# Linear attention on one core: the remainder from keys times state, and the block inverse applied to it

## What is computed

```python
DN_HEADS, DN_DK, DN_DV, DN_CHUNK = 8, 128, 128, 64
a = jnp.where(strict, beta[..., :, None] * kk * decay, 0.0) + jnp.eye(DN_CHUNK)
rhs = jnp.concatenate([beta[..., None] * v, (beta * jnp.exp(g))[..., None] * k], axis=-1)
sol = lax.linalg.triangular_solve(a, rhs, left_side=True, lower=True, unit_diagonal=True)
u_t, w = sol[..., :dv], sol[..., dv:]
attn = jnp.einsum('bhnid,bhnjd->bhnij', q, k) * decay
q_g = q * jnp.exp(g)[..., None]
k_d = k * jnp.exp(g_last[..., None] - g)[..., None]

def step(state, xs):
    u_tc, w_c, attn_c, qg_c, kd_c, gl_c = xs
    u = u_tc - jnp.einsum('bhcd,bhde->bhce', w_c, state)
    o = jnp.einsum('bhcd,bhde->bhce', qg_c, state) + jnp.einsum('bhij,bhje->bhie', attn_c, u)
    state = jnp.exp(gl_c)[..., None, None] * state + jnp.einsum('bhcd,bhce->bhde', kd_c, u)
    return state, o
```

## Time and profile before

| what | value |
|---|---|
| median of 3 runs | 1782.01 us |
| the 3 runs | 1780.25, 1787.84, 1782.01 us |
| span of the profiled execution | 1783.6 us |
| PE busy | 1706.6 us (96%) |
| DVE busy | 703.0 us (39%) |
| ACT busy | 465.0 us (26%) |
| POOL busy | 140.3 us (8%) |
| turning of values of head 0 to head 7 (L711, first and last) | 179.3 to 344.1 us from the span's start |
| PE waits for a DMA of expert weights, both layers | 21.5 us in 29 waits |

### The profile page before, as it was taken

How to read it: one execution, slowest core, us unless ns; L and a number is a source line. 1 busy time by engine, 2 the same in 40 slices (tenths; PEclk the granted TensorE clock), 3 DMA queues, 4 the chain that set the end, 5 groups by cost and what they waited for, 6 DMA issues and landing times. The chain is left out here.

```text
span 1783.6 us, 19887 instructions
## 1 busy us (share of the span) xinstructions
PE 1706.6 (96%) x7340; PEld 829.5 (47%) x7340; DVE 703.0 (39%) x1365; ACT 465.0 (26%) x709; POOL 140.3 (8%) x192
## 2 busy tenths in 40 slices
PE   7999999998999999999998999989899999999998
PEld 4555666643334434433345565565343443433343
DVE  4788444415333433333322103355333433333231
ACT  5666244412101011000124716653101101001020
POOL 0035710000000000000000101100000000000000
PEclk9999999999999999999999999999899999999999
DMA  8122232385999999999951020045899999999941
GB/s 280 51 81 74 79 83 71 110 326 201 426 426 427 426 426 427 427 427 429 410 217 48 1 103 0 1 189 218 346 427 426 427 427 426 427 427 429 427 168 47
DMA packets 85113, 481.06 MB, mean 270 GB/s; under 512 B 22320, under 2 KB 39472, under 8 KB 58416
## 3 DMA queue, kind: packets, MB, share of 16 engines
q1 hardware_dynamic: 80432, 471.64, 65.0%
q0 software_dynamic: 4608, 8.40, 1.3%
HBM read 476.33 MB, written 12.06 MB: 274 GB/s over the span
## 5 line engine op out<-in xcount | busy, mean ns | idle before, releaser
L1937 PE MATMUL bank<-ring,xT 128*64 128x512 f32 x2048 | 465.2, 600 | 22.2 <-DMA ring<-in_w 21.5
L1937 PEld LDWEIGHTS bank<-ring,xT 128*64 128x64 f32 x2048 | 142.4, 137 | 289.1 <-issue 272.0
L1889 DVE TENSOR_TENSOR H<-H,bank 128x512 f32<-128x512 f32 x240 | 154.0, 683 | 301.8 <-PE bank L1925 301.8
L1961 PE MATMUL bank<-ring,sg 128*64 128x512 f32 x1024 | 228.3, 598 | 0.3 <-ACT sg L1977 0.2
L1961 PEld LDWEIGHTS bank<-ring,sg 128*64 128x64 f32 x1024 | 70.8, 137 | 134.3 <-issue 126.3
L635 PE MATMUL bank<-ring,ring 128*128 128x512 f32 x256 | 126.9, 604 | 0.0
L620 PE MATMUL bank<-ring,ring 128*128 128x512 f32 x256 | 112.9, 593 | 0.0
L1977 ACT ACTIVATE sg<-bank 128x512 f32<-128x512 f32 x32 | 19.2, 600 | 353.1 <-PE bank L1946 353.1
L1879 DVE SCALAR_TENSOR_TENSOR low<-bank,weight_now,high 128x512 fp32r<-128x512 f32 x64 | 48.1, 751 | 159.3 <-ACT high L1983 156.0
L2305 PE MATMUL bank<-ring,ring 128*128 128x512 f32 x256 | 110.5, 592 | 0.0
L1925 PE MATMUL bank<-high,Sb 128*128 128x512 f32 x240 | 106.7, 445 | 0.0
(11 more groups left out here) (336 smaller groups left out, 2024.6 us busy)
## 6 DMA issues: line engine op xcount, KB each, us to landing
ring<-in_w SPq DMA_DIRECT2D x192, 2048.0 KB, 30.2
ring<-in_w_heads SPq DMA_DIRECT2D x16, 1024.0 KB, 5.1
ring<-in_w_ple_gate SPq DMA_DIRECT2D x4, 2048.0 KB, 32.9
ring<-in_w_kv SPq DMA_DIRECT2D x3, 2048.0 KB, 21.3
ring<-in_b_w_q SPq DMA_DIRECT2D x3, 2048.0 KB, 19.6
inverses<-ring SPq DMA_DIRECT2D x16, 256.0 KB, 4.1
ring<-inverses SPq DMA_DIRECT2D x16, 256.0 KB, 3.2
rows<-ring SPq DMA_DIRECT2D x8, 512.0 KB, 4.3
```

Of the source, the lines that this page charges most:

```text
L1889: dve.tensor_tensor(out, out, k.bank[6 + j % 2][:, :], ALU.add).then_inc(s.added, 1)
L1937: last = pe.matmul(out[e * SLOTS:(e + 1) * SLOTS, :], k.xT[:, at, e * SLOTS:(e + 1) * SLOTS], w[:, e, c, :], start=(at == 0), stop=(at == ...
L1961: last = pe.matmul(k.bank[2 + n][e * SLOTS:(e + 1) * SLOTS, :], k.hT[:, c, e * SLOTS:(e + 1) * SLOTS], w[:, e, c % 2, n * HALF:(n + 1) * H ...
```

## The change

The product W of inverse and scaled keys goes, with its copy nWT and with kb. In tile t > 0 TensorE multiplies the plain normalised keys by the state (L745 of the changed program, into bank 2, semaphore kS), VectorE adds that, times -beta e^g of the token, to vb (`remainder`, one 128x128 op, semaphore r), and V is applied to the result. A filler stands between the product and V's. beG gets its sign when it is made. The normalised keys are written to oT, whose slot of a head is free until that head's output is written, in place of the qk buffer. Wait for ln_o (ScalarE has read bank 2) joins the wait for og, and both stand ahead of tile 0.

```diff
@@ delta_semaphores, early_units
-     s.Z, s.Ts, s.W, s.nW, s.u, ...
+     s.Z, s.Ts, s.kS, s.r, s.u, ...
-                pe.wait_ge(s.nW, HEADS)
+                pe.wait_ge(s.tok, 2 * HEADS)
                 yield from unit(3, range(HEADS - 1))
@@ TensorE, keys
-                q, kk = k.qk[:, h % 2, 0, :], k.qk[:, h % 2, 1, :]
+                q, kk = k.qk[:, h % 2, 0, :], k.oT[:, h, :]
@@ TensorE, recur
-                pe.wait_ge(s.tok, 3 * h + 3)
+                pe.wait_ge(s.tok, 2 * h + 2)
                 pe.wait_ge(s.Vs, JOINS * h + JOINS)
+                wait(pe, s.og, h)
+                wait(pe, s.ln_o, h)
                 for t in range(NT):
-                    last = pe.matmul(tile(bank[6], t), k.kb[:, t, :], V[:, t, :], start=True, stop=True)
-                last.then_inc(s.W, 1)
-                wait(pe, s.og, h)
-                for t in range(NT):
-                    last = pe.matmul(tile(bank[3], t), V[:, t, :], k.vb[:, t, :], start=True, stop=(t == 0),
-                                     skip_group_check=True)
                     if t:
-                        pe.wait_ge(s.nW, h + 1)
                         pe.wait_ge(s.St, 3 * h + t)
-                        last = pe.matmul(tile(bank[3], t), tile(k.nWT[:, :], t), k.state[:, (t - 1) % 2, :],
-                                         start=False, stop=True, skip_group_check=True)
-                    last.then_inc(s.u, 1)
+                        pe.matmul(tile(bank[2], t), tile(k.oT[:, h, :], t), k.state[:, (t - 1) % 2, :], start=True,
+                                  stop=True).then_inc(s.kS, 1)
+                        take(rest, 1)
+                        pe.wait_ge(s.r, 3 * h + t)
+                    pe.matmul(tile(bank[3], t), V[:, t, :], k.vb[:, t, :], start=True, stop=True).then_inc(s.u, 1)
                     take(rest, 1)
                     pe.wait_ge(s.us, 4 * h + t + 1)
@@ VectorE
-                dve.tensor_tensor(kk, kk, k.rnorm[:, 1, :], ALU.mult).then_inc(s.qkn, 1)
+                dve.tensor_tensor(k.oT[:, h, :], kk, k.rnorm[:, 1, :], ALU.mult).then_inc(s.qkn, 1)
...
-                wait(dve, s.W, h)
...
-                for dst, scale in ((k.kb, k.beG), (k.kd, k.eGrest)):
-                    dve.tensor_tensor(dst[:, :, :], k.kt[:, h, :, :], bcast(head_of(scale, h), 2, P),
-                                      ALU.mult).then_inc(s.tok, 1)
+                dve.tensor_tensor(k.kd[:, :, :], k.kt[:, h, :, :], bcast(head_of(k.eGrest, h), 2, P),
+                                  ALU.mult).then_inc(s.tok, 1)
...
+            def remainder(h, t):
+
+                dve.wait_ge(s.tok, 2 * h + 2)
+                dve.wait_ge(s.kS, 3 * h + t)
+                dve.scalar_tensor_tensor(k.vb[:, t, :], tile(bank[2], t), head_of(k.beG, h)[:, t:t + 1], k.vb[:, t, :],
+                                         ALU.mult, ALU.add).then_inc(s.r, 1)
...  (recur, at the end of each of the three rounds that make a state)
+                    remainder(h, t + 1)
@@ ScalarE, recur
-                act.wait_ge(s.W, h + 1)
-                act.activation(k.nWT[:, :], bank[6][:, :], ACT.Copy, scale=-1.0).then_inc(s.nW, 1)
```

More of the change, by code:

```diff
@@ L515, in gates_vector_sums @@
                       k.bank[3][:, NT * HEADS:2 * NT * HEADS], G, ALU.subtract).then_inc(g.diff, 1)
-    ch.link(dve.tensor_tensor(k.beG[:, :, :], k.beta[:, :, :], k.eG[:, :, :], ALU.mult))
+    ch.link(dve.scalar_tensor_tensor(k.beG[:, :, :], k.beta[:, :, :], -1.0, k.eG[:, :, :], ALU.mult, ALU.mult))
     dve.wait_ge(g.acts, 2)
@@ L544, in delta_semaphores @@
      s.exported, s.blocks, s.init, s.inv, s.flipped, s.returned, s.C, s.tok, s.v_turned, s.X, s.Xs, s.Y, s.Vs,
-     s.Z, s.Ts, s.W, s.nW, s.u, s.us, s.dS, s.St, s.o, s.osq, s.oss, s.ln_o, s.rn_o, s.og_step, s.og, s.low, s.olow, s.w_late) = (
+     s.Z, s.Ts, s.kS, s.r, s.u, s.us, s.dS, s.St, s.o, s.osq, s.oss, s.ln_o, s.rn_o, s.og_step, s.og, s.low, s.olow, s.w_late) = (
          k.sem(f"dn_{name}") for name in
@@ L549, in delta_semaphores @@
              "zeroed", "exported", "blocks", "init", "inv", "flipped", "returned", "C", "tok", "v_turned",
-             "X", "Xs", "Y", "Vs", "Z", "Ts", "W", "nW", "u", "us", "dS", "St", "o", "osq", "oss", "ln_o",
+             "X", "Xs", "Y", "Vs", "Z", "Ts", "kS", "r", "u", "us", "dS", "St", "o", "osq", "oss", "ln_o",
              "rn_o", "og_step", "og", "low", "olow", "w_late"))
@@ L796, in _ @@
                 last.then_inc(done, 1)
-            R.free[2], R.free[4] = (s.tok, 3 * HEADS), (s.C, JOINS * HEADS)
+            R.free[2], R.free[4] = (s.tok, 2 * HEADS), (s.C, JOINS * HEADS)
             R.free[3] = R.free[5] = (s.o, HEADS)
@@ L2644, in build @@
             k.C = part(4, 2).rearrange("p (l t n) -> p l t n", l=JOINS, t=NT)
-            k.kb, k.kd, k.vb, k.us = (four(part(at, 1)) for at in (9, 10, 1, 2))
+            k.kd, k.vb, k.us = (four(part(at, 1)) for at in (10, 1, 2))
             k.X = part(0, 1)[:, 0:NT * P // 2]
-            k.nWT, k.osq, k.og = (part(at, 1) for at in (3, 6, 7))
+            k.osq, k.og = (part(at, 1) for at in (6, 7))
             def prefetch_first(sp, dead, load_last, spent):
```

## The result

The changed kernel takes 1801.26 us (median of 4 runs, 1799.46 to 1801.86); the kernel before, with one more run beside it, 1784.87 us (1780.25 to 1787.84). The ratio is 1.0086, 95% interval 1.0072 to 1.0100: slower by 13 to 18 us. The forecast was 1792.2 us with a range of 1782 to 1799. The direction came out and both forecast pauses are there; the size did not come out, and a fall of the clock came on top that the sum held at nothing. The profiled execution's span went from 1783.6 to 1799.4 us, +15.8.

A forecast was written before the change was run, and what follows sets the result against it. TensorE's queue was taken to pace the recurrence; 0.6 us at the first head boundary plus 6 x 1.6 = 9.6 at the others gave +10.2 on 1782.01, so 1792.2 us, 8-in-10 range 1782 to 1799.

The forecast's parts named there:

- both forecast pauses: TensorE idle per head: about 1 us ahead of V times vb (og), about 1.6 us ahead of the turning (silu).
- What bounds the kernel: TensorE's queue paces the recurrence, 23.28 us per head; og's wait and silu's at the head's end are only just met.
- W at zero gain: Ahead of tile 0: removing W's 0.88 us gains nothing in heads 1 to 7, since it lay under og's wait.
- The round trip covered: Tiles 1 to 3: product to remainder takes 0.83 us, under 1.08 us of cover, 0.25 to spare; zero cost.
- The moved fillers: Head's end: three fillers moved into tiles make the last product 2.58 us later; TensorE idles 1.6 us per head.
- tied: Head's end: convolution ends 1.49 us and squares 1.51 us behind the last product's start; no extra cost, no cover.
- Head 0 to head 1: First boundary: product Y comes 0.5 to 1.0 us later through VectorE's queue, taken as 0.6, head 0's gain included.
- the start after a wait: TensorE's first product behind a wait: 0.06 us after the releasing op, taken from V times vb behind og.
- The rival that I took for all or nothing: the clock: New idle stretches lower TensorE's clock: +7 us for one fall per head, up to twice that, 1799 to 1806; chance 0.09.
- The row that I set against it: Experts' stretch: PE idles 4.45 us of 60 in short pieces at clock 1.00, cited against a clock fall.
- the rival it came from: W's time is really won, both waits covered: 8 x 0.88 = 7.0 us faster, 1775 us; chance 0.08.

The follow-up runs named there:

- e2: Changed kernel plus four unused 128x128 products per head where W stood; 1797.29 us, ratio 1.0070.
- e6: Changed kernel with VectorE's two output ops put ahead of the last subtraction of the joins, so og comes sooner; 1788.68 us, ratio 1.0021.
- e9: Kernel before, keeping W, nWT, kb and fillers, with VectorE's output ops ahead of the last subtraction and silu ahead of the squares; 1782.53 us, ratio 0.9987.
- e8: Changed kernel with the edits of e6 and e7 together, and og waited for last; 1780.41 us, ratio 0.9972.
- e3: Changed kernel without the filler between keys times state and V; three fillers back at the head's end; 1807.17 us, ratio 1.0108.
- e10: The kernel of e8 run again, on the same chip as e9; 1780.66 us, ratio 0.9983.
- e5: Changed kernel plus 1.3 us of matmuls with unread results ahead of the wait for silu at the turning; 1797.02 us, ratio 1.0064.
- e4: Changed kernel with the waits for ln_o and og in the other order, og last; 1800.02 us, ratio 1.0077.
- e1: Kernel before with only a third filler in tiles 1 to 3, W, nWT and kb kept; 1798.7 us, ratio 1.0069.
- e7: Changed kernel with the convolution's four ops spread over VectorE's gaps in tiles 2 and 3, and silu ahead of the squares; 1788.96 us, ratio 1.0019.

## Why the prediction was right or wrong

- *What bounds the kernel: right.* Both places named, og's wait ahead of tile 0 and the end of the head, are where the idle time is: of TensorE's waits from 205 to 375 us these two make 16.5 us, one other 0.7.
- *W at zero gain: right.* e2 puts the products back and the head gets no longer. e6 and e9 against e8 show the other side: with og out of the way, their 0.9 us is there to be had.
- *The round trip covered: right,* and the margin was fair: r's chain is 0.07 us longer than taken (0.49 and not 0.42 from product to op), out of the 0.25 to spare. That costs nothing. e3 shows what the cover is worth.
- *The moved fillers: right in kind, sized 1.6 us per head, measured 1.67* from V times vb to the next turning (358.15 - 342.28 = 15.87, before 274.05 - 259.85 = 14.20). Most of that 0.07 is the later start behind silu, the next term but one. The convolution (to 355.98) and the squares (to 356.02) tied, as said.
- *Head 0 to head 1: right.* From head 0's turning to the product Y of head 1 it is 206.42 - 178.78 = 27.64 us in the changed profile, 206.36 - 179.35 = 27.01 before: +0.63, forecast 0.6.
- *The term that was too small: the start after a wait.* I took 0.06 us from one place, V times vb behind og (259.79 to 259.85). In the changed kernel that start takes 0.26, and the turning's behind silu 0.15. How long TensorE had been idle is not what sets it: behind the remainder in e3 it is 0.06 after 0.51 us of idle, behind the copy of X in e10 0.06 after 1.10, and behind silu 0.15 after 0.23 (e5) as after 1.53. What goes with it is the waits that stand directly ahead of the product. With one wait alone (og in the kernel before, r, Xs) it is 0.05 to 0.06; where the wait that is met last stands behind another (silu, og in e4) 0.14 to 0.15; where a further wait stands behind it (og ahead of ln_o) mostly 0.26. e2, with og and ln_o ahead of the product and 0.06, doesn't fit, so the cause stays open. Tile 0 so starts 9.30 us after the turning instead of 9.08. These 0.22 and the 0.07 of the moved fillers make a head cost 1.89 and not 1.6, 1.4 us over the five heads after the second boundary. The change itself put four waits where one stood, and the sum had no term for that.
- *The rival that I took for all or nothing: the clock.* The sum had the clock at nothing, and I gave 0.09 to a fall in every head. It fell in two of seven, 1.65 us each, 3.3 us, and this is the largest single miss of the forecast. That the falls cost this is in the rows; that the pauses make them is only likely. e5, with the pause filled, has no falls and 25.17 us in heads 2 to 6, but e6 has six unfilled pauses and no fall either. The Trainium skill (TensorE: Matmul & The Clock Gate, the section on a second failure mode) tells of another kernel, at bf16, whose many micro-idles made the clock swing; the traces of the changed kernel and of e1, e2, e3 and e4 agree with that, and e6's doesn't. The row that I set against it, the experts' stretch in the earlier trace rows, has idles of up to 1.2 us and heavy work between, and was no fair witness for 1.5 us ahead of small products.
- *The range.* The layer was forecast at 10.2; it cost 11.6 for the pauses and 3.3 for the clock, and 1.3 came behind it. The kernel before also came out 2.6 to 4 us higher in later runs than the 1782.01 that I started from, 2.9 in the result. Of the 9.1 us between forecast and measurement these four (1.4, 3.3, 1.3, 2.9) make 8.9. A case "falls in some heads" belonged between the forecast and the full rival. And the chances held a slip: 0.07 stood for faster by more than 8.9 us, while the rival it came from was worth 7.0.

## What to carry to other kernels

Where a saturated engine waits for nothing, look for the work that merely stands in front of a wait which is about to end: taking it away yields nothing, until the wait is moved too. Independent matmuls spread as cover are a fixed stock; a new round trip that takes three of them must be weighed against the place they came from, and here the cheaper answer was to move the late chains (e6, e7) and not the cover. Count the waits ahead of a product on the critical path, and put the one that is met last at the end. The clock may fall behind some idle pieces of 1.5 us and not behind others, so price a partial fall, not only none or all.

## What the runs showed of the hardware

TensorE's first product behind a wait starts 0.05 to 0.06 us after the releasing op's end where that wait stands alone, after idles of 0.46 to 1.10 us; 0.14 to 0.15 behind silu's wait, after idles of 0.17 to 1.53 us; and mostly 0.26 behind og's when ln_o's stands after it, 0.11 more than in the other order (e4). Pauses of 1.5 us once per head go with falls of the clock to the 1.2 GHz level in one or two heads of the changed kernel, e1, e2 and e4, and with none in e6. VectorE's new op, with one operand in PSUM, took 349 to 352 ns, beside POOL's work and without it; the Trainium skill (SBUF — State Buffer, on the shared port pair) says that an op with at most one input in SBUF, outside the two-port modes, does not contend with GpSimd, and the trace agrees. VectorE's op on two tensors in SBUF that otherwise takes 0.68 us took 2.47 and 2.48 us beside one copy of POOL (e10, e9).
